# A hybrid decoder step: where value pages land, in which turn pages are requested, and where heads stand beside the key pages

## The chip, the cores and the metric

The kernel runs on one core of a Trainium2 chip. The metric is device time in microseconds (us) of one execution, from the first instruction to the end of the last. TensorE (PE) multiplies, VectorE (DVE) and ScalarE (ACT) work elementwise, GpSimd (POOL) does a little arithmetic and requests the cache pages, SyncE (SP) requests the weights; 16 DMA engines move what all of them request. Each engine runs its own instructions strictly in order and waits on semaphores.

## The reference

A decoder trunk of four layers is run for a prompt of 256 tokens and for 8 sample sequences of one token each. Layer 1 mixes tokens by block-sparse attention, layer 2 by a gated linear recurrence. Cut to what the change touches:

```
def moba_mixer(xn, pos0, w_qkv, w_o, k_pool, v_pool, li, table):
    q, k, v = jnp.split(xn @ w_qkv, 3, axis=-1)      # 8 heads of 128
    ...  # top 3 past blocks of 256 keys by q . mean(k), and the own block
    s = jnp.einsum('bqhd,bqhkld->bqhkl', qg, kg).astype(jnp.float32) * scale
    s = jnp.where(mask, s, -jnp.inf).reshape(b, qb, H, n_slots * MOBA_BLOCK)
    p = jax.nn.softmax(s, axis=-1).reshape(b, qb, H, n_slots, MOBA_BLOCK).astype(vg.dtype)
    return jnp.einsum('bqhkl,bqhkld->bqhd', p, vg)
    ...
    return out @ w_o, k, v

def rglru_mixer(xn, conv_buf, h0, w_in, conv_w, conv_b, w_a, b_a, w_x, b_x, lam, w_out):
    gate_br, x_br = jnp.split(xn @ w_in, 2, axis=-1)
    x_br, new_buf = causal_dwconv(x_br, conv_buf, conv_w, conv_b)
    r = jax.nn.sigmoid(jnp.einsum('blnc,ncd->blnd', xb, w_a) + b_a).reshape(b, L, LRU_WIDTH)
    i = jax.nn.sigmoid(jnp.einsum('blnc,ncd->blnd', xb, w_x) + b_x).reshape(b, L, LRU_WIDTH)
    a = jnp.exp(-LRU_C * r * jax.nn.softplus(-lam))
    ...  # h = a h + sqrt(1 - a^2) i x, then gelu(gate_br) * h @ w_out
```

Each sample sequence has 8 cache pages of 128 rows and 8 heads of 128, for keys and again for values: 64 key pages and 64 value pages of 0.5 MB each.

## The kernel before

**Projections.** Every weight matrix is taken in chunks of 1024 x 256 (1 MB). SP loads a chunk into one of four buffers `raw0` to `raw3`; ACT copies it to a high part `whi`, DVE subtracts to a low part `wlo` (two buffers each, `split`, L1009 and L1612); PE does 48 matmuls on it (L549 to L551). Of the output projection `wo`, chunks 0 and 1 wait in `raw0` and `raw1` and are split while the attention runs, by the two splits named `split(stage[1, "qkv"], 2, ...)`; SP loads chunks 2 and 3 into `raw2` and `raw3` after value page 31 was used.

**The sample group's attention.** Call the key pages K0 to K63 and the value pages V0 to V63, eight to a sequence. POOL requests each with one DMA (L1508) after it has read its number from the page table. A key page lands in one of the eight buffers `pg0` to `pg7`. DVE multiplies half of it by the sequence's query row and multiplies and sums the other half (`key_scores`, L1980 and L1982); ACT sums the first half in place (`key_sums`, L1215). The buffer is free when both are through (semaphores `s_kd`, `s_ka`). The query row is spread over the partitions by PE (`query`, L779); from the fifth sequence on, all share one PSUM bank, so query n waits until K(8n-1) is through. After K31 comes the first softmax (sequences 0 to 3: `scores_T`, `block_parts`, `exponentials`, `normalised`, `shares_T`, `spread`), after K63 the second. The result are the shares `pm`. PE multiplies them by four value pages at a time (`quad`, L863, 16 quads), the first eight after the first softmax, the others after the second; `s_vd` counts used value pages. `summed` and `gather` (L1251, L873) bring each half's sum into place.

**The prompt's attention** runs one head at a time beside it: `front` on PE (L832, L833; transposes of keys and values and the scores), `scores` on DVE (starts with the copy at L2061), `weigh` on ACT (L1240, L1241), `shares` on DVE (starts with L2073), `weights_T` on PE (L512 out of `sc`), `turned` on ACT (L1247), `head_sum` on PE (L848, L849), `head_out` on DVE (L2080). `front` of a head waits for `scores` of the head before.

All of this stands in an order written out by hand: for each engine a loop over the pages, with tables that say at which page which step of which head is run.

**Where value pages land before.** V0 to V31 go round eight buffers, four in `raw2` and `raw3` (`pgr`) and four of their own (`pgx`); V32 on go round the eight key buffers and the four `pgx`. POOL requests V0 to V7, then K24 to K39 without a value between them, then K40, V8, K41, V9 and so on to K63, V31, then V32 to V63 as buffers come free.

**The recurrence layer.** The input projection is 8 chunks: four for the gate branch, four for x. Behind each of the last four DVE scales the result (`XR`, L2180), convolves two tiles (L2191, L2194) and PE multiplies them by the gate weights (`gates`, L917, L918); ACT takes tanh (`gate_tanh`), DVE forms log a (`log_a`), ACT its exponentials (`decay_parts`), then DVE scans.

## Time and profile before

| | us |
|---|---|
| median of 3 runs | 2012.89 |
| lowest and highest | 2010.73, 2019.34 |
| the profiled execution | 2013.81 |
| its span of instructions | 2011.8 |

Busy shares of the span: PE 90%, DVE 66%, ACT 47%, POOL 25%. They are averages: through most of the span PE multiplies without a pause. The two stretches that the change touches are not like that. The attention runs from about 661 us (last matmul of the qkv projection) to 857.7 us (first matmul of the `wo` projection), the end of the recurrence layer's input from about 1139 to 1193 us. Times inside the trace count from the span's start.

### The profile page before, as it was taken

What the parts mean: (1) busy time and instruction counts of PE and PEld (TensorE: products, weight loads), DVE (VectorE), ACT (ScalarE), POOL (GpSimd) and SP (SyncE); (2) the same over time, 40 slices, a digit from 0 to 9 for tenths busy, and PEclk for the clock granted to TensorE, in tenths of its full rate; (3) what the DMA queues carried; (4) which work ended last, traced back from release to release, by engine and by line L of the source; (5) the groups of instructions that cost most, each with busy time, mean ns of one, the idle gap of its engine ahead of it and who ended that gap; (6) DMA issues with size and microseconds to landing.
All of it is one profiled execution on the core that took longest, in us unless ns stands there. A gap on an engine that the chain in (4) does not pass through costs nothing.

```text
span 2011.8 us, 35750 instructions
## 1 busy us (share of the span) xinstructions
PE 1807.4 (90%) x13437; PEld 1650.6 (82%) x13437; DVE 1334.8 (66%) x2470; ACT 948.6 (47%) x1713; POOL 504.1 (25%) x424
## 2 busy tenths in 40 slices
PE   4999989999999265799999859999999998999996
PEld 4999758999999121399999859999989875899996
DVE  4998796654575876465556876544799879655554
ACT  2546664453344655245434454533454666445333
POOL 2500500441120323234211005411150050144111
PEclk9999988999999667999999979999999998999998
DMA  5454494655557879955554507555546439465540
GB/s 179 132 175 135 112 264 139 195 188 169 179 172 234 324 286 387 335 161 179 177 167 154 184 2 241 185 179 170 155 135 184 134 111 265 132 199 184 180 154 22
DMA packets 317970, 365.04 MB, mean 181 GB/s; under 512 B 7802, under 2 KB 290978, under 8 KB 317750
## 3 DMA queue, kind: packets, MB, share of 16 engines
q1 hardware_dynamic: 296068, 287.41, 45.4%
q0 software_dynamic: 20560, 74.62, 10.0%
q8 instruction: 76, 1.25, 0.3%
q10 hardware_dynamic: 1216, 1.35, 0.2%
q14 instruction: 50, 0.41, 0.1%
HBM read 340.79 MB, written 23.15 MB: 181 GB/s over the span
## 4 chain that ended last, share of the span: by engine, by line
PE 62%; DVE 17%; issue 8%; ACT 5%; DVEq 3%; POOLq 2%; DMA 2%; POOL 1%; ACTq 1%; SPq 0%
PE G L549 17%; PE G L550 17%; PE G L551 17%; DVE wlo L1612 5%; ACT whi L1009 2%; DVE sums L1920 2%; PE A L512 2%; DVE xbc L1768 1%; PE A L863 1%; POOLq L1507 1%; PE A L965 1%; DVEq L1770 1%; PE G L663 1%; PE A L654 1%; DVE stx L1912 1%
## 5 line engine op out<-in xcount | busy, mean ns | idle before, releaser
L1612 DVE TENSOR_TENSOR wlo<-raw,whi 128x2048 fp32r<-128x2048 f32 x234 | 548.2, 2343 | 330.0 <-ACT whi L1009 329.9
L1009 ACT ACTIVATE whi<-raw 128x2048 fp32r<-128x2048 f32 x234 | 447.9, 1914 | 571.8 <-PE G L551 567.9
L549 PE MATMUL G<-xH,whi 128*128 128x264 f32 x2112 | 605.5, 287 | 25.6 <-DVE xL L1674 12.7
L550 PE MATMUL G<-xH,wlo 128*128 128x264 f32 x2112 | 600.3, 284 | 0.0
L551 PE MATMUL G<-xL,whi 128*128 128x264 f32 x2112 | 599.9, 284 | 0.0
L549 PEld LDWEIGHTS G<-xH,whi 128*128 128x128 f32 x2112 | 399.6, 189 | 35.7 <-issue 18.5
L550 PEld LDWEIGHTS G<-xH,wlo 128*128 128x128 f32 x2112 | 399.9, 189 | 0.1
L551 PEld LDWEIGHTS G<-xL,whi 128*128 128x128 f32 x2112 | 398.0, 188 | 0.0
L549 PE MATMUL G<-aH,whi 128*128 128x264 f32 x1024 | 292.2, 285 | 7.9 <-DVE wlo L1612 7.9
L550 PE MATMUL G<-aH,wlo 128*128 128x264 f32 x1024 | 290.7, 284 | 0.0
L551 PE MATMUL G<-aL,whi 128*128 128x264 f32 x1024 | 290.7, 284 | 0.0
L1574 POOL TENSOR_TENSOR ac<-rl 128x528 f32<-128x528 f32 x64 | 167.4, 2615 | 203.3 <-ACT rl L1343 203.3
L549 PEld LDWEIGHTS G<-aH,whi 128*128 128x128 f32 x1024 | 193.5, 189 | 9.0 <-DVE wlo L1612 9.0
L550 PEld LDWEIGHTS G<-aH,wlo 128*128 128x128 f32 x1024 | 193.7, 189 | 0.0
L551 PEld LDWEIGHTS G<-aL,whi 128*128 128x128 f32 x1024 | 192.7, 188 | 0.0
L1422 POOL TENSOR_TENSOR sums<-h 128x528 f32<-128x528 f32 x27 | 39.2, 1453 | 325.1 <-DVE xg L1664 324.8
L1420 POOL TENSOR_TENSOR sums<-h 128x528 f32<-128x528 f32 x9 | 17.5, 1945 | 362.1 <-DVE xg L1664 362.1
L1215 ACT ACTIVATE pg<-pg 128x128 f32<-128x128 f32 x256 | 75.7, 297 | 61.9 <-DVE pg L1980 60.7
L1768 DVE SCALAR_TENSOR_TENSOR xbc<-T,colC,xbc 128x256 f32<-128x256 f32 x192 | 98.4, 553 | 7.5 <-ACT xbc L1091 2.3
L2243 DVE TENSOR_TENSOR aL<-ac,aH 128x528 f32 (+1 forms) x64 | 45.3, 708 | 66.7 <-POOL ac L1574 65.6
L549 PE MATMUL G<-yH,whi 128*128 128x264 f32 x256 | 75.2, 294 | 7.8 <-DVE yL L1949 5.7
L549 PE MATMUL G<-pH,whi 128*128 128x264 f32 x256 | 75.8, 296 | 0.0
(426 smaller groups left out, 3067.1 us busy)
## 6 DMA issues: line engine op xcount, KB each, us to landing
raw<-in_mlp_w_up SPq DMA_DIRECT2D x64, 1024.0 KB, 5.3
raw<-in_mlp_w_down SPq DMA_DIRECT2D x64, 1024.0 KB, 5.1
raw<-in_ssd_w_in SPq DMA_DIRECT2D x48, 1024.0 KB, 5.4
pg<-in_cache_k POOLq DMA_DIRECT2D x64, 512.0 KB, 5.7
raw<-in_ssd_w_out SPq DMA_DIRECT2D x16, 1024.0 KB, 7.6
raw<-in_ple_w_gate SPq DMA_DIRECT2D x16, 1024.0 KB, 5.1
raw<-in_moba_w_qkv SPq DMA_DIRECT2D x12, 1024.0 KB, 5.2
pgx<-in_cache_v POOLq DMA_DIRECT2D x24, 512.0 KB, 5.9
```

The costliest lines, as they stand in the source:

```text
L512: return nc.tensor.transpose(out, in_, ident[0:k, 0:k])
L549: mm(o, whi[u % 2][:, k, w], act_h[:, x, :], start=first, stop=False)
L550: mm(o, wlo[u % 2][:, k, w], act_h[:, x, :], start=False, stop=False)
L551: done = mm(o, whi[u % 2][:, k, w], act_l[:, x, :], start=False, stop=last)
L1009: fn(whi[u % 2][:], raw[(u + 2) % 4][:], ACT.Copy).then_inc(s_hi, 1)
L1215: f = fn(pg[f"pg{j}"][:, hh, :], pg[f"pg{j}"][:, hh, :], ACT.Copy, accum_out=ms[f"sq{n % 2}"][:, j, hh:hh + 1])
L1422: gp.tensor_tensor(hh2, hr, hr, ALU.mult)
L1574: gp.tensor_tensor(ml[f"ac{b}"][:], ml[f"rl{b}"][:], ml[f"rl{b}"][:], ALU.mult).then_inc(s_ac, 1)
L1612: V.tensor_tensor(wlo[u % 2][:], raw[(u + 2) % 4][:], whi[u % 2][:].bitcast(F32), ALU.subtract).then_inc(s_lo, 1)
L1768: f = V.scalar_tensor_tensor(o, T_[:, t, k:k + SEQ], colC[:, q, ds(tile + k * CT, 1)], o, ALU.mult, ALU.add)
L1920: f = V.tensor_tensor_reduce(spare[:, (t % 8) * P:(t % 8 + 1) * P], stx[k][:, t, :], bank[t // 8][:, (t // 2 % 4) * P:(t // 2 % 4 + 1) * P ...
L2243: V.tensor_tensor(aL[:, ds(r * 2, 2), :], ml[f"ac{b}"][:], aH[:, ds(r * 2, 2), :].bitcast(F32), ALU.subtract).then_inc(s_aL, 1)
```

## The change

- Sixteen early value buffers: eight new ones, `pgw0` to `pgw7`, lie over the split buffers `whi` and `wlo`, then the four `pgr` and the four `pgx`. V0 to V47 and V56 to V63 go round these sixteen, V48 to V55 lie in the key buffers.
- Four semaphores for landed values, one for four pages, take the place of one for `pgr` and four for `pgx`.
- From K24 on POOL requests keys and values in turns: K24, V0, K25, V1 to K63, V39, then V40 to V63.
- The two early splits of `wo` stand at heads 6 and 7 and wait until V35 (ACT) and V39 (DVE) were used. SP loads chunks 2 and 3 of `wo` after V59.
- PE's order around the quads is written out anew. Five heads, not four, have their scores and shares before the second softmax; their steps stand at other pages on DVE and ACT.
- In the recurrence layer `gates` and `gate_tanh` of a pair stand one chunk later, and the first `log_a` stands behind the last convolution.

```
```diff
@@ -205,8 +206,10 @@
+        pgw = [nc.alloc_sbuf_tensor_at(f"pgw{k}", [P, MH, P], F32, offset=w0 + 4 * MH * P * k) for k in range(8)]
+        early = [t[:] for t in pgw] + pgr + [t[:] for t in pgx]
@@ -352,15 +354,9 @@
-            if t < 32:
-                turn, k = t // 8, t % 8
-                if k < 4:
-                    return pgr[k], s_pv, 64 * (turn + 1)
-                return pgx[k - 4][:], s_px[k - 4], 16 * (turn + 1)
-            turn, k = (t - 32) // RING, (t - 32) % RING
-            if k < PAGES:
-                return pg[f"pg{k}"][:], s_pg[k], 16 * (NB + turn + 1)
-            return pgx[k - PAGES][:], s_px[k - PAGES], 16 * (4 + turn + 1)
+            if 48 <= t < 56:
+                return pg[f"pg{t - 48}"][:], s_pg[t - 48], 16 * (NB + 1)
+            return early[t % 16], s_pv[t // 4 % 4], 64 * (t // 16 + 1)
@@ -472,10 +468,9 @@
-                        if hh == 3:
-                            sp.wait_ge(s_vd, 32)
-                            load_one(stage[1, "wo"], 2)
-                            load_one(stage[1, "wo"], 3)
+                    sp.wait_ge(s_vd, 60)
+                    load_one(stage[1, "wo"], 2)
+                    load_one(stage[1, "wo"], 3)
@@ -875,23 +870,52 @@
                 scores_T(0)
                 query(4)
                 shares_T(0)
-                for i in range(2 * NB):
-                    if i in (3, 5, 7, 9, 11, 13, 15):
-                        head_sum({3: 0, 5: 1, 7: 2, 9: 3, 11: 4, 13: 5, 15: 6}[i])
-                    if i in (2, 4, 6, 8, 10, 12, 14, 15):
-                        weights_T({2: 0, 4: 1, 6: 2, 8: 3, 10: 4, 12: 5, 14: 6, 15: 7}[i])
-                    if i in (1, 3, 5, 7, 9, 10, 12, 14):
-                        front({1: 0, 3: 1, 5: 2, 7: 3, 9: 4, 10: 5, 12: 6, 14: 7}[i])
-                    if i == 7:
-                        scores_T(1)
-                    if i == 8:
-                        shares_T(1)
-                    if i == 13:
-                        gather(0)
-                    quad(i)
-                    if i in (1, 3, 5):
-                        query(5 + i // 2)
-                head_sum(MH - 1)
+                quad(0)
+                front(0)
+                quad(1)
+                quad(2)
+                query(5)
+                weights_T(0)
+                quad(3)
+                head_sum(0)
+                front(1)
+                quad(4)
+                query(6)
+                weights_T(1)
+                quad(5)
+                head_sum(1)
+                front(2)
+                quad(6)
+                query(7)
+                weights_T(2)
+                quad(7)
+                head_sum(2)
+                front(3)
+                weights_T(3)
+                head_sum(3)
+                front(4)
+                weights_T(4)
+                scores_T(1)
+                head_sum(4)
+                front(5)
+                shares_T(1)
+                quad(8)
+                weights_T(5)
+                quad(9)
+                head_sum(5)
+                front(6)
+                quad(10)
+                weights_T(6)
+                quad(11)
+                head_sum(6)
+                front(7)
+                gather(0)
+                quad(12)
+                weights_T(7)
+                quad(13)
+                head_sum(7)
+                quad(14)
+                quad(15)
@@ -919,12 +943,12 @@
                 def after_in(it, u):
                     states(it, u)
-                    if not is_first(it) and u:
-                        gates(2 * u - 2)
-                        gates(2 * u - 1)
+                    if not is_first(it) and u > 1:
+                        gates(2 * u - 4)
+                        gates(2 * u - 3)
                 project(stage[2, "lru_in"], xH, xL, norm=6, after=after_in)
-                gates(KT - 2)
-                gates(KT - 1)
+                for n in range(4, KT):
+                    gates(n)
@@ -1254,21 +1278,24 @@
                     for hh in range(4):
-                        if t == (38, 46, 54, 62)[hh]:
+                        if t == (37, 42, 50, 57)[hh]:
                             weigh(hh)
-                        if t == (42, 50, 58, -1)[hh]:
+                        if t == (39, 44, 52, 59)[hh]:
                             turned(hh)
-                split(stage[1, "qkv"], 2, 2)
+                    if t == 61:
+                        weigh(4)
+                    if t == 62:
+                        turned(4)
                 exponentials(1)
-                turned(3)
-                for hh in range(4, MH):
+                for hh in range(5, MH):
                     weigh(hh)
-                    if hh == 4:
-                        split(stage[1, "qkv"], 2, 3)
                     turned(hh)
-                    if hh == 4:
+                    if hh == 5:
                         act.wait_ge(s_pr, 10)
                         summed(0)
+                    if hh > 5:
+                        act.wait_ge(s_vd, 36)
+                        split(stage[1, "qkv"], 2, hh - 4)
@@ -1308,12 +1335,14 @@
-                    if u:
-                        gate_tanh(2 * u - 2)
-                        gate_tanh(2 * u - 1)
+                    if u > 1:
+                        gate_tanh(2 * u - 4)
+                        gate_tanh(2 * u - 3)
+                gate_tanh(4)
+                gate_tanh(5)
                 decay_parts(0)
-                gate_tanh(KT - 2)
-                gate_tanh(KT - 1)
+                gate_tanh(6)
+                gate_tanh(7)
                 decay_parts(1)
...
                     act.wait_ge(s_lv, n + 1)
@@ -1513,20 +1542,13 @@
-                def value_early(turn, k):
-                    if not (isinstance(turn, int) and turn == 0):
-                        pool.wait_ge(s_vd, turn * 8 + (k - 7))
-                    buf, landed, _ = value_slot(k)
-                    page(t_in["cache_v"], turn * 8 + k, buf, landed)
-                def value_late(t):
-                    if t < 32 + PAGES:
-                        pool.wait_ge(s_kd, t + 25)
-                        pool.wait_ge(s_ka, t + 25)
-                    else:
-                        pool.wait_ge(s_vd, t - RING + 1)
+                def value_page(t):
+
+                    if 48 <= t < 56:
+                        pool.wait_ge(s_kd, t + 9)
+                        pool.wait_ge(s_ka, t + 9)
+                    elif t >= 16:
+                        pool.wait_ge(s_vd, t - 15)
                     buf, landed, _ = value_slot(t)
                     page(t_in["cache_v"], t, buf, landed)
@@ -1534,23 +1556,16 @@
                 with gp.Fori(1, 3) as it:
                     for j in range(PAGES):
                         key_page(it, j)
+                pool.wait_ge(s_mm, stage[1, "qkv"]["g0"] + 12)
                 pool.wait_ge(s_lo, stage[1, "wo"]["g0"])
-                for k in range(4):
-                    value_early(0, k)
-                pool.wait_ge(s_mm, stage[1, "qkv"]["g0"] + 12)
-                for k in range(4, 8):
-                    value_early(0, k)
-                for j in range(PAGES):
-                    key_page(3, j)
-                gp.memset(pm[:], 0.0).then_inc(s_pm, 1)
-                for j in range(PAGES):
-                    key_page(4, j)
-                with gp.Fori(1, 4) as it:
+                for n in range(3, NB):
                     for j in range(PAGES):
-                        key_page(it + 4, j)
-                        value_early(it, j)
-                for t in range(32, NB * PAGES):
-                    value_late(t)
+                        key_page(n, j)
+                        value_page(8 * (n - 3) + j)
+                    if n == 3:
+                        gp.memset(pm[:], 0.0).then_inc(s_pm, 1)
+                for t in range(40, NB * PAGES):
+                    value_page(t)
@@ -2087,25 +2102,29 @@
                     for hh in range(4):
-                        if t == (37, 45, 53, 61)[hh]:
+                        if t == (36, 41, 49, 56)[hh]:
                             scores(hh)
-                        if t == (38, 46, 54, 62)[hh]:
+                        if t == (38, 43, 51, 58)[hh]:
                             shares(hh)
-                        if t == (47, 55, -1, -1)[hh]:
+                        if t == (42, 50, 57, 60)[hh]:
                             head_out(hh)
+                    if t == 60:
+                        scores(4)
+                    if t == 62:
+                        shares(4)
                 block_parts(1)
-                head_out(2)
+                head_out(4)
+                scores(5)
                 normalised(1)
                 spread(1)
+                shares(5)
                 ov = ms["ov"][:].rearrange("p (b h) -> p b h", h=MH)
-                head_out(3)
-                for hh in range(4, MH):
+                for hh in range(6, MH):
+                    head_out(hh - 1)
                     scores(hh)
-                    if hh > 4:
-                        head_out(hh - 1)
                     shares(hh)
-                    if hh < 6:
-                        split(stage[1, "qkv"], 2, hh - 2)
+                    dve.wait_ge(s_vd, 40)
+                    split(stage[1, "qkv"], 2, hh - 4)
                 head_out(7)
@@ -2183,8 +2202,6 @@
                     if u == 0:
...
-                    if u == 3:
-                        log_a(0)
@@ -2194,6 +2211,7 @@
                 dve.drain()
+                log_a(0)
                 log_a(1)
...
```

Three places in the order. PE, behind the fourth page row of `query(5)`: L779 is the query in the kernel before, then the transposes of head 0's shares, a quad (its eight rows stand as "..."), `head_sum`, and `front(1)`. Before:

```order
L779 MATMUL A<-rowS,ident 128x512 [waits s_kd]
L779 MATMUL A<-rowS,ident 128x512
L512 MATMUL G<-ident,sc_130 128x128 [waits s_mP]
L512 MATMUL G<-ident,sc_130 128x128 x2
...
L848 MATMUL G<-pt_131,kvt_129 128x256 [waits s_mpt]
L849 MATMUL G<-pt_131,kvt_129 128x128
L512 MATMUL G<-ident,qkv 128x128 [waits s_msc]
L512 MATMUL G<-ident,qkv 128x128 x3
L832 MATMUL G<-qkv 128x128
L833 MATMUL G<-qkv 128x256
```

PE now has the same rows in the same turn, with the quad out of other buffers; only two quads, not one, stand between `front(0)` and the query. So `front(1)` stands as far behind the query as it did. What moved is its reader on DVE. DVE before, from the second key page of sequence 5 on (K41): after the copy of the sums comes K42, and `scores(1)` stands only behind K45.

```order
L1980 TENSOR_TENSOR pg_122<-pg_122,A 128x512 [waits s_pg1]
L1982 ISA pg_122,sq_154<-pg_122,A 128x128
...
L1995 COPY sS<-sq_153 128x8x8 [waits s_ka]
L1980 TENSOR_TENSOR pg_123<-pg_123,A 128x512 [waits s_pg2]
L1982 ISA pg_123,sq_154<-pg_123,A 128x128
```

DVE now, from the same page (the lines have other numbers; L2076 is the copy that begins `scores`):

```order
L1995 TENSOR_TENSOR pg_122<-pg_122,A 128x512 [waits s_pg1]
L1997 ISA pg_122,sq_154<-pg_122,A 128x128
...
L2010 COPY sS<-sq_153 128x8x8 [waits s_ka]
L2076 COPY kvt_136<-G 128x512 [waits s_mtp]
L2077 TENSOR_TENSOR sc_137<-G,amask 128x384
L2079 TENSOR_REDUCE mx_139<-sc_137 128x1
L2080 TENSOR_REDUCE mx_139<-sc_137 128x1
L2082 TENSOR_SCALAR nm_140<-mx_139 128x2
L1995 TENSOR_TENSOR pg_123<-pg_123,A 128x512 [waits s_pg2]
```

`scores(1)` stands right behind K41 and waits (`s_mtp`) for the `front(1)` that PE runs seven steps behind the query.

PE in the recurrence layer, behind the last chunk of the input projection: before, gates 4 and 5 and then 6 and 7, of which each waits for its convolution (`s_lc`).

```order
L917 MATMUL A<-xc,wax 128x264 [waits s_lth,s_lc]
L918 MATMUL A<-xc,wax 128x264
L917 MATMUL A<-xc,wax 128x264 [waits s_lth,s_lc]
L918 MATMUL A<-xc,wax 128x264
L917 MATMUL A<-xc,wax 128x264 [waits s_lth,s_lc]
```

Now gates 2 to 7 stand there in one row (twelve matmuls), 0 and 1 stand behind the chunk before, and none behind the second x chunk:

```order
L941 MATMUL A<-xc,wax 128x264 [waits s_lth,s_lc]
L942 MATMUL A<-xc,wax 128x264
L941 MATMUL A<-xc,wax 128x264 [waits s_lth,s_lc]
L942 MATMUL A<-xc,wax 128x264
L941 MATMUL A<-xc,wax 128x264 [waits s_lth,s_lc]
L942 MATMUL A<-xc,wax 128x264
```

## Rows read from the trace of the kernel before

**Rows 1.** Windows of 20 us: busy us of each engine, clock, DMA share.

```profile
core 0: us, PE busy (x) PEld busy (x) DVE busy (x) ACT busy (x) POOL busy (x), PEclk, DMA share, GB/s
700.00:720.00 20.00, 8.77 (x34) 4.29 (x38) 15.12 (x82) 11.30 (x63) 3.69 (x7) 0.50 0.61 234
...
760.00:780.00 20.00, 13.20 (x51) 4.16 (x45) 14.43 (x82) 11.22 (x70) 7.46 (x15) 0.84 1.01 390
```

**Rows 2.** Timeline of POOL's page requests (start, us, instruction, idle before): V0, K24, K40, V56.

```profile
677.21 0.53 POOL L1508 DMA_DIRECT2D raw<-in_cache_v  x1 [0.78 <-issue]
...
686.78 0.53 POOL L1508 DMA_DIRECT2D pg<-in_cache_k  x1 [0.70 <-issue]
...
717.78 0.53 POOL L1508 DMA_DIRECT2D pg<-in_cache_k  x1 [10.28 <-issue]
...
830.50 0.53 POOL L1508 DMA_DIRECT2D pg<-in_cache_v  x1 [0.64 <-issue]
```

**Rows 3.** Groups by line, 661 to 858 us: ACT's sums over key pages.

```profile
L1215 ACT ACTIVATE pg<-pg 128x128 f32<-128x128 f32 x224 | 66.2, 296 | 48.6 <-DVE pg L1980 47.8
```

**Rows 4.** Timeline of DVE: K24, first shares, K40, K41, scores(1), shares(1), K48, K63, second shares.

```profile
693.00 0.69 DVE L1980 TENSOR_TENSOR pg<-pg,A 128x512 f32<-128x512 f32 x1 [7.91 <-DMA pg<-in_cache_k]
...
718.34 0.62 DVE L2050 COPY pm<-G 128x64 f32<-128x64 f32 x4 [0.22 <-PE G L823]
...
735.67 0.69 DVE L1980 TENSOR_TENSOR pg<-pg,A 128x512 f32<-128x512 f32 x1 [3.87 <-PE A L779]
...
737.10 0.68 DVE L1980 TENSOR_TENSOR pg<-pg,A 128x512 f32<-128x512 f32 x1
...
744.54 0.68 DVE L2061 COPY kvt<-G 128x512 f32<-128x512 f32 x1
...
749.42 0.17 DVE L2073 RECIPROCAL ri<-rs 128x2 f32<-128x2 f32 x1 [1.39 <-ACT sc L1241]
...
754.80 0.69 DVE L1980 TENSOR_TENSOR pg<-pg,A 128x512 f32<-128x512 f32 x1 [2.82 <-PE A L779]
...
793.72 0.68 DVE L1980 TENSOR_TENSOR pg<-pg,A 128x512 f32<-128x512 f32 x1
...
807.98 0.61 DVE L2050 COPY pm<-A 128x64 f32<-128x64 f32 x4 [1.58 <-PE A L823]
```

**Rows 5.** Timeline of PE: scores_T(0), query(5), weights_T, quad, head_sum, front, quads, gather(1), wo.

```profile
705.94 1.89 PE L512 MATMUL G<-ident,sS 128*32 128x128 f32 x8 [28.99 <-DVEq L1989]
...
731.85 3.78 PE L779 MATMUL A<-rowS,ident 8*128 8x512 f32 x4 [6.66 <-DVE sq L1982]
735.56 0.90 PE L512 MATMUL G<-ident,sc 128*128 128x128 f32 x3
737.88 3.67 PE L863 MATMUL A<-raw,pm 128*32 128x512 f32 x16 [1.42 <-DMA raw<-in_cache_v]
741.48 1.04 PE L848 MATMUL G<-pt,kvt 128*128 128x256 f32 x2
...
743.76 1.49 PE L863 MATMUL A<-pgx,pm 128*32 128x512 f32 x6
...
815.03 1.94 PE L863 MATMUL A<-pg,pm 128*32 128x512 f32 x16
...
853.99 2.82 PE L873 MATMUL A<-headsel,vO 128*128 128x4 f32 x16 [3.57 <-ACT vO L1251]
857.74 0.59 PE L549 MATMUL G<-oH,whi 128*128 128x264 f32 x1 [0.93 <-DVE oL L2121]
```

**Rows 6.** Timeline of PE in the recurrence layer: the first gate.

```profile
1148.60 1.25 PE L917 MATMUL A<-xc,wax 128*128 128x264 f32 x2 [4.14 <-DVE xc L2194]
```

**Rows 7.** Timeline of DVE there: first and last log_a.

```profile
1166.27 1.15 DVE L2175 TENSOR_SCALAR la<-thr,ch 128x264 f32<-128x264 f32 x4
...
1175.84 0.36 DVE L2175 TENSOR_SCALAR la<-thr,ch 128x264 f32<-128x264 f32 x1 [1.40 <-ACT thi L1286]
```

**Rows 8.** Timeline of ACT there: the first of three decay instructions of the second half.

```profile
1176.23 1.08 ACT L1299 ACTIVATE thr<-la 128x1056 f32<-128x1056 f32 x1 [0.42 <-DVE la L2175]
```

4 lines of the change are left out of this document (2 added, 2 removed).

## The prediction

> **What bounds the kernel now.** I read the windows of 20 us first, then the timelines of POOL, DVE and PE between 661 and 858 us, then the end of the recurrence layer's input. Most of the span is PE multiplying, and the change doesn't touch it. Two stretches are different.
>
> In the attention a window in mid-stretch shows every DMA engine full at 390 GB/s [rows 1], so a page of 524,288 bytes costs 1.34 us of the queue. The window from 700 us has a DMA share of 0.61 and 234 GB/s [rows 1]: there POOL has nothing that it may request. It stood 10.28 us before K40, whose buffer is held by K32, and K32 waits for the first softmax [rows 2]. Further holes follow later, since V44 on want buffers that only the second half's quads free; V56, of the last eight, is requested at 830.50 [rows 2], 22 us after the second shares at 807.98 [rows 4]. DVE is the other candidate: a key page costs it 1.43 us (735.67 to 737.10), and 64 are to be done, with the heads between them [rows 4]. Its waits are the reading that matters: 7.91 us for K24, 3.87 us and 2.82 us for the query at K40 and K48 [rows 4]. Between K40 and K48 it needed 19.13 us, where the queue delivers eight keys and eight values in 16 x 1.34 = 21.4. So neither is far ahead of the other: from the first shares to K63 they take turns. Behind the second shares comes 857.74 - 808.6 = 49.1 us until `wo` begins [rows 4, 5]: four heads in a row, eight quads and the last pages.
>
> In the recurrence layer PE stands 4.14 us before the first gate [rows 6], and the last `log_a` waits for tanh at 1175.84 [rows 7].
>
> **The change part by part.** I follow each engine's turn from page to page with the durations of the rows; hand-overs between engines, 0.1 to 0.2 us, are in the differences of starts that I use.
>
> *Requests in turns from K24.* V0 to V7 no longer go ahead of K24. K24 is requested where V0 was, at 677.2 instead of 686.8 [rows 2], so the 7.91 us of DVE's wait [rows 4] go. Not all is gained: K25 to K31 now come at every second place of the queue. K24 landed as the ninth page from 677.2 at 692.9; K31 is now the fifteenth, at 692.9 + 6 x 1.34 = 701.0, so DVE ends it at 702.4. Before, it ended about 0.9 us ahead of the first transposes at 705.94 [rows 5], at 705.1. Gain 2.7 us; the first shares move from 718.3 to 715.6. K39, the 31st page, lands at 722.4, ahead of its turn.
>
> *Sixteen buffers.* V0 to V15 land in the hole before K40. From there keys and values alternate at 1.34 us each; V16 on wait for quads that PE has run long before. By this row the queue reaches V47 about 798 and V55 about 809, some 14 us ahead of the second half's quads. So the values are no longer late, and what is late next is DVE with PE.
>
> *`scores(0)` one page earlier and `shares(0)` behind K38.* The 1.39 us that DVE waits for the exponentials [rows 4] shrink to some 0.3, part of it taken by `front(0)`: 0.7 us more. The query for sequence 5 comes 2.7 + 0.7 = 3.4 us earlier and DVE starts K40 at 735.7 - 3.4 = 732.3.
>
> *`scores` right behind the query.* Here the change adds a wait. `scores(1)` stands behind K41, 2 x 1.43 + 0.1 = 3.0 us after the query. It needs `front(1)`, and PE has to run before it, at 1.2 GHz, `weights_T` 0.90, a quad 3.67, `head_sum` 1.04 [rows 5]; then `front` itself 1.2 (from the end of `head_sum` at 742.5 to 743.76). That is 6.8, with hand-overs 7.0. DVE stands 4.1 us, all key pages queued behind it. Before, `scores(1)` stood behind K45 at 744.54 and did not wait [rows 4]. The period K40 to K48 is then 19.13 - 1.39 (no wait for the exponentials) + 0.6 (the query 3.4 instead of 2.82) + 4.1 = 22.4 us. The next is the same with `scores(2)` behind K49: K56 starts at 732.3 + 2 x 22.4 = 777.1. The third hold is longer, since `scores(3)` stands behind K56 alone: 7.0 - 1.4 = 5.6. For K56 to K63 I sum 8 x 1.43 = 11.4, hold 5.6, two `scores` of 2.0 (the copy at 744.54 to the next key page), two `shares` of 0.7, two `head_out` of 0.4, the collect 0.1, and 1.6 for waits on `head_sum(3)` and `front(4)` (PE's `weights_T(3)` can only follow `shares(3)` behind K58): 24.9, with hand-overs 25.7. K63 ends at 802.8, before at 793.72 + 1.43 = 795.15: **7.6 us later**, although it started 3.4 earlier.
>
> *ACT's `turned(1)` at K44* waits for `weights_T(1)`, which PE runs only after query 6, so behind K47. The sums of K45 to K47 (four at 0.296 us, 1.18 a page [rows 3]) come 4 to 5 us late, and K53's request with them. The queue is idle as long; K53 lands about 764 and is used about 769. I cost it at nothing; the lead of 5 us is the cover.
>
> *The second softmax.* K63's end to the last copy of shares took 13.4 us (795.15 to 808.6). `scores(5)`, 2.0 us, stands where DVE waited for the exponentials, and `head_out(4)` with it: I add 1.0. Second shares at 802.8 + 14.4 = 817.2, 8.6 us later than before.
>
> *Behind it three heads, not four, and no page to wait for.* A quad costs 3.67 at 1.2 GHz and 1.94 at 2.4 GHz [rows 5]. From the shares: quad 8 3.7, `weights_T(5)` 0.9, quad 9 half and half 2.6, `head_sum` 0.9, `front(6)` 1.2, to 9.3; the DVE and ACT part of head 6, 4.2 (744.54 to 749.42, less the key page of 1.43, plus `shares` 0.7 [rows 4]), to 13.5, with quad 10 beside it; `weights_T` 0.5, quad 11 1.9, `head_sum` 0.9, `front(7)` 1.2, gather 1.8, quad 12 1.9, to 21.7; head 7's shares are ready at 23.2 because DVE's split of 2.3 us stands before its scores; `weights_T` 0.5, quad 13 1.9, `head_sum` 0.9, quads 14 and 15 3.9, to 30.4; then the copy of the sums 1.0, the gather 1.8 (2.82 before, at 1.2 GHz), and the last three small steps 2.1 with hand-overs, to 35.3. `wo` begins at 852.5, before at 857.74 [rows 5]: **gain 5.2 us**. PE comes out of it with a gap of 2 us, not 3.57 [rows 5], so I give its first chunk 1.2 us for 2.4 GHz at once (between 0 and 1.9).
>
> *Later loads of `wo`.* Chunks 2 and 3 are requested after quad 14, at about 846, and land by 852; needed from 858. Cost nothing, 5 to 6 us of cover; the two splits of chunks 0 and 1 are done by 845.
>
> *Recurrence layer.* Chunk 6 follows chunk 5 at once, 4.14 us earlier, and a `log_a` with its product, 2.3 us, leaves DVE's path before the last convolution. The convolutions end about 6 us earlier. ACT takes part back: tanh of gates 2 to 7 come in one row behind the last `XR`, and the first half's decays (three of 1.08 [rows 8]) stand before tanh 6 and 7. The last `log_a` comes at 1172.1, not 1175.84 [rows 7]: **gain 3.8 us** (2 to 6).
>
> Sum on the profiled execution: 2013.8 - 5.2 - 1.2 - 3.8 = 2003.6. It was 0.9 above the median of the runs, so 2002.7, say 2003.
>
> The Trainium skill, page "Perfetto Trace Analysis", section "Identifying the Most-Contended Engine", says to work first on the engine with the highest occupancy. In this stretch that would be the transfers, and this change would take nearly all their idle time away. That gives the third rival below, which stands on rows without it.
>
> **The rivals.**
>
> *The holds don't come* (faster). If PE reaches 2.4 GHz soon after the query, a quad is 1.94 and the whole row to `front` about 5, not 7; and DVE may be later than I think at K41. All three holds gone are 13.3 us, two thirds 9. Time 2003 - 11 = 1992. For it: the quad at 815.03 ran at 1.94. Against: at each query of the trace of before PE had stood idle for some us, 6.66 before the fifth, and its quad behind it took 3.67 [rows 5].
>
> *Clock low throughout* (slower). PE has only short bursts between DVE's and ACT's steps, so it may stay at 1.2 GHz all along: each hold grows by 1.8 (slower `front`, `query` at 3.8), and behind the second shares six quads on the path cost 1.7 more each, the two gathers 1.0 each. 5.4 + 10.2 + 2 = 17.6 over the forecast, 2020. It decides from the point where the second shares come after 827, or where the quads of the last eight take over 3 us. For it: the window from 700 us has clock 0.50 [rows 1]. Against: 1.94 in the same place of the kernel before.
>
> *The queue decides* (much faster): 104 pages from 677 at 1.34 give the last at 692.9 + 95 x 1.34 = 820, and `wo` at 827, 31 us early: 1977. Against: V56 to V63 wait for quads 10 and 11.
>
> *Nothing from the attention*: K53 to K55 land late after all (the 5 us lead used up), or chunk 2 of `wo` does, since the next weights are loaded at once behind it; either takes the 5 to 6 us. 2003 + 6 = 2009: within 0.5%.
>
> **How the numbers follow.** Forecast 0.42, its own range 1998 to 2009; no holds 0.25, at 1992; queue 0.04; nothing from the attention 0.15, at 2009; clock low 0.14, around 2020, half of it over 2023. About 0.5% (10 us) is what a measurement of this kernel tells from no change: the borders are 2002.8 and 2023. Faster: half the forecast's 0.42 and the 0.29 of the two fast rivals, 0.50. Slower: 0.08. The rest, 0.42, is within. From 1988 to 2018 leaves out the queue, the far half of the slow rival and the far edge of the fast one.
>
> **What would show it.** Right: DVE idle 3 to 6 us before the copies of `scores(1)`, `(2)`, `(3)`, released by PE's `front`; no wait for K24; V40 on requested without a hole to V55; second shares near 817; `wo` begun near 852; PE without 4.14 us before the first gate. Wrong: holds under 2 us (shares before 810, total under 1995); shares after 825; a wait of DVE on pages K53 to K56; a wait of PE on chunk 2 of `wo`.

## The result, and the profile after

The changed kernel takes 2001.85 us (median of 7 runs, 2000.76 to 2006.14), the kernel before beside it 2015.74 (7 runs, 2010.73 to 2019.34). The ratio, estimated from all runs of both kernels and not from the two medians (which alone would say 0.9931), is 0.9938, with a 95% interval of 0.9922 to 0.9953: 12.5 us less, 9 to 16. I had predicted 2003 and a gain of 10. The profiled run took 2006.14 with a span of 2004.4, the longest of the seven, so its span (7.4 under the 2011.8 of before) shows less than the ratio does.

The first timeline is that of DVE, from K27 to the second shares. Columns as in [rows 4]: start, us, instruction, and the idle time before it with what ended it.

```profile
691.47 0.69 DVE L1995 TENSOR_TENSOR pg<-pg,A 128x512 f32<-128x512 f32 x1 [1.04 <-DMA pg<-in_cache_k]
...
701.71 0.69 DVE L1995 TENSOR_TENSOR pg<-pg,A 128x512 f32<-128x512 f32 x1 [1.04 <-DMA pg<-in_cache_k]
...
716.48 0.62 DVE L2065 COPY pm<-G 128x64 f32<-128x64 f32 x4 [0.22 <-PE G L818]
...
733.31 0.69 DVE L1995 TENSOR_TENSOR pg<-pg,A 128x512 f32<-128x512 f32 x1 [3.87 <-PE A L774]
...
740.22 0.69 DVE L2076 COPY kvt<-G 128x512 f32<-128x512 f32 x1 [3.67 <-PE G L828]
...
756.14 0.69 DVE L1995 TENSOR_TENSOR pg<-pg,A 128x512 f32<-128x512 f32 x1 [3.87 <-PE A L774]
...
760.99 0.20 DVE L2010 COPY sS<-sq 128x64 f32<-128x64 f32 x1 [1.91 <-ACT pg L1239]
...
761.93 0.69 DVE L2076 COPY kvt<-G 128x512 f32<-128x512 f32 x1 [0.74 <-PE G L828]
...
784.49 0.69 DVE L2076 COPY kvt<-G 128x512 f32<-128x512 f32 x1 [5.48 <-PE G L828]
...
817.21 0.62 DVE L2065 COPY pm<-A 128x64 f32<-128x64 f32 x4 [1.58 <-PE A L818]
```

What to see: the 7.91 us before K24 in [rows 4] are gone, with five waits of 1.04 us (K27 to K31) in their place. K40 starts 2.4 us earlier (733.31, before 735.67). `scores(1)`, the first L2076 copy behind it, waits 3.67 us for PE's `front` (L828); `scores(2)` waits 0.74 behind a wait of 1.91 for ACT's sums, `scores(3)` 5.48. The second shares come at 817.21, 9.2 us later than in [rows 4].

PE's timeline around query 5 shows where 3.67 us come from:

```profile
729.50 3.77 PE L774 MATMUL A<-rowS,ident 8*128 8x512 f32 x4 [3.60 <-DVE sq L1997]
733.21 0.90 PE L507 MATMUL G<-ident,sc 128*128 128x128 f32 x3
734.03 3.66 PE L858 MATMUL A<-pgx,pm 128*32 128x512 f32 x16
737.63 1.22 PE L843 MATMUL G<-pt,kvt 128*128 128x256 f32 x2
...
739.58 0.60 PE L828 MATMUL G<-qkv 128*128 128x256 f32 x2
```

PE stands idle for 3.60 us until K39 is through, makes the query, and then does `weights_T(0)`, a quad and `head_sum(0)` before the `front(1)` for which DVE waits.

POOL's requests of V16, K53 and V56, and PE at the end of the attention:

```profile
721.59 0.53 POOL L1537 DMA_DIRECT2D pgw<-in_cache_v  x1 [4.72 <-issue]
...
759.89 0.53 POOL L1537 DMA_DIRECT2D pg<-in_cache_k  x1 [7.63 <-ACT pg L1239]
...
828.57 0.53 POOL L1537 DMA_DIRECT2D raw<-in_cache_v  x1 [18.10 <-issue]
```

```profile
848.29 1.95 PE L868 MATMUL A<-headsel,vO 128*128 128x4 f32 x16 [1.84 <-ACT vO L1275]
851.17 0.42 PE L544 MATMUL G<-oH,whi 128*128 128x264 f32 x1 [0.93 <-DVE oL L2140]
```

`wo` begins at 851.17, 6.6 us before the 857.74 of [rows 5]. From the second shares on it takes 34.0 us, before 49.8. (Both count from the start of the copies of the shares; the prediction counted from their end, 808.6 before and 817.8 now.) In the recurrence layer DVE's last `log_a` is this:

```profile
1165.36 0.36 DVE L2194 TENSOR_SCALAR la<-thr,ch 128x264 f32<-128x264 f32 x1 [0.39 <-ACT thi L1313]
```

### The profile page after: what moved, and what is told of

It reads as the page before. It is cut to its first block, busy times and chain, and to the rows that moved or that the text cites. A ratio compares the mean times of both kernels' runs of the same rounds, so it can differ in the third digit from the quotient of the medians.

```text
span 2004.4 us, 35656 instructions
## 1 busy us (share of the span) xinstructions
PE 1796.1 (90%) x13437; PEld 1649.9 (82%) x13437; DVE 1334.7 (67%) x2470; ACT 947.1 (47%) x1713; POOL 504.0 (25%) x424
## 3 DMA queue, kind: packets, MB, share of 16 engines
q8 instruction: 76, 1.25, 0.3%
## 4 chain that ended last, share of the span: by engine, by line
PE 62%; DVE 19%; issue 7%; ACT 5%; DVEq 3%; DMA 1%; POOLq 1%; ACTq 1%; POOL 0%; SPq 0%
PE G L544 17%; PE G L545 17%; PE G L546 16%; DVE wlo L1627 5%; ACT whi L1033 3%; DVE sums L1935 2%; PE A L507 2%; DVE xbc L1783 1%; PE A L989 1%; PE A L858 1%; DVE pg L1997 1%; DVE pg L1995 1%; DVEq L1785 1%; PE G L507 1%; PE G L658 1%
## 5 line engine op out<-in xcount | busy, mean ns | idle before, releaser
L544 PE MATMUL G<-xH,whi 128*128 128x264 f32 x2112 | 605.1, 286 | 26.6 <-DVE wlo L1627 13.6
L544 PEld LDWEIGHTS G<-xH,whi 128*128 128x128 f32 x2112 | 399.6, 189 | 36.6 <-issue 18.6
L544 PE MATMUL G<-aH,whi 128*128 128x264 f32 x1024 | 292.2, 285 | 8.0 <-DVE wlo L1627 8.0
L544 PEld LDWEIGHTS G<-aH,whi 128*128 128x128 f32 x1024 | 193.5, 189 | 9.1 <-DVE wlo L1627 9.0
L1239 ACT ACTIVATE pg<-pg 128x128 f32<-128x128 f32 x256 | 75.5, 297 | 48.9 <-DVE pg L1995 48.3
L544 PE MATMUL G<-yH,whi 128*128 128x264 f32 x256 | 75.3, 294 | 7.8 <-DVE yL L1964 5.7
L544 PE MATMUL G<-pH,whi 128*128 128x264 f32 x256 | 75.8, 296 | 0.0
```

Source lines behind the costliest of these rows:

```text
L544: mm(o, whi[u % 2][:, k, w], act_h[:, x, :], start=first, stop=False)
L1239: f = fn(pg[f"pg{j}"][:, hh, :], pg[f"pg{j}"][:, hh, :], ACT.Copy, accum_out=ms[f"sq{n % 2}"][:, j, hh:hh + 1])
```

## The experiments

All are compared with the kernel before, run beside them. For the attention I use two differences inside one trace, since the stretch ahead of it varies between executions (in the profiled runs query 4 starts between 670.5 and 674.9 us): the times from the start of query 4 on PE (673.17 before, 673.25 after) to the first shares, the second shares and the first matmul of `wo`. The recurrence layer's part adds nothing to them. us:

| kernel | first shares | second shares | `wo` | shares to `wo` | ratio |
|---|---|---|---|---|---|
| before | 45.2 | 134.8 | 184.6 | 49.8 | 1 |
| after | 43.2 | 144.0 | 177.9 | 34.0 | 0.9938 |
| x1, attention alone | 42.6 | 143.3 | 177.3 | 34.0 | 0.9969 |
| x2, recurrence alone | 46.0 | 135.2 | 185.5 | 50.3 | 0.9977 |
| x6, buffers and requests | 42.5 | 130.0 | 178.0 | 48.0 | 0.9954 |
| x3, turned later | 42.8 | 143.8 | 177.7 | 34.0 | 0.9949 |
| x4, fronts first | 43.1 | 134.0 | 168.9 | 34.9 | 0.9902 |
| x5, both of these | 42.8 | 133.6 | 167.7 | 34.1 | 0.9894 |
| x7, x5 with scores at query | 43.6 | 135.1 | 169.9 | 34.9 | 0.9886 |
| x8, x5 with keys first | 37.7 | 133.1 | 168.0 | 34.9 | 0.9893 |
| x9, x7 with K41, K42 ahead | 43.0 | 131.9 | 166.6 | 34.7 | 0.9870 |
| x10, x5 with the old buffers | 45.3 | 159.8 | 205.4 | 45.6 | 1.0060 |

**The two parts by themselves.** x1 is the changed kernel with the recurrence layer as before, x2 the kernel before with the recurrence layer's part of the change (gates one chunk later, both `log_a` behind the last convolution).

> The changed kernel with the recurrence layer as before, so only the attention part of the change. Theory (the parts add up): the attention stage ends 6.6 us earlier than before, as in the trace of the changed kernel (first wo matmul at 851.2 instead of 857.7 us), some 0.4 us of it is given back in the projection, and the time is 6 us under before, near 2009 where before is 2015. Rival (the recurrence part carries the gain): 0 to 2 us under before.

> The kernel before with the recurrence layer's gates and first log_a moved, and nothing else. Theory: last log_a 4.4 us earlier relative to the layer's start, as in the changed kernel (forecast 3.8), and the time 4 to 5 us under before. Rival: the gain of PE's 4.14 us wait is given back by ACT, whose tanh come in one row: under 2 us.

x1 gave 0.9969 (0.9958 to 0.9980), 6.2 us, x2 0.9977 (0.9964 to 0.9989), 4.6 us. Their product is 0.9946, within the interval of the whole change: the parts add. Inside the traces the recurrence layer gains 4.4 us: from the start of its input projection (1110.60 before, 1104.52 now, 1108.70 in x2) to the last `log_a` it takes 65.2 us before, 60.8 in the changed kernel and 60.9 in x2. One trace of each is a rough measure: in x1, whose recurrence layer is that of before, the same stretch took 67.1.

**Buffers and requests without the fifth head.** The changed kernel (its recurrence layer too) with PE's loop as before and four heads ahead of the second softmax at the places of before, on DVE and ACT. On DVE:

```
-                        if t == (36, 41, 49, 56)[hh]:
+                        if t == (37, 45, 53, 61)[hh]:
                             scores(hh)
...
-                        if t == (42, 50, 57, 60)[hh]:
+                        if t == (47, 55, -1, -1)[hh]:
                             head_out(hh)
```

> The changed kernel's sixteen buffers, requests in turns, late splits and late wo loads, and its recurrence layer, but with the order of PE's quads and heads and the pages at which DVE and ACT run the heads' steps as before (four heads ahead of the second softmax). Theory (the request part gains, the order of the heads gives part of it back): key pages end near 789 us, second shares near 802, and then four heads of about 9 us take wo to begin near 846, 5 us earlier than in the changed kernel. Rival (the fifth head ahead is what gains): wo begins at 856 or later, no better than before but for the recurrence layer.

It gave 0.9954 (0.9937 to 0.9970), and from query 4 to `wo` 178.0 us, where the changed kernel takes 177.9. The theory held up to the second shares (802.03), and missed behind them: 48.0 us, not 44, so the order of the heads gives nothing back and brings nothing. The fifth head and the new order take 14.0 us off what lies behind the second shares and put 14.0 us in front of them. So what the attention gains (0.9969 in x1) is, as far as one trace of each can tell, all from the buffers and requests; how much of it is the sixteen buffers and how much the turns of the requests was not tried apart. What they removed can be read in the trace of before: DVE waited there for the key pages K53 and K58 to K61, 4.3 us together, and PE 1.42, 4.20 and 6.90 us for the value pages of quads 2, 4 and 6. Two of these rows of DVE before:

```profile
763.49 0.69 DVE L1980 TENSOR_TENSOR pg<-pg,A 128x512 f32<-128x512 f32 x1 [1.02 <-DMA pg<-in_cache_k]
...
785.70 0.69 DVE L1980 TENSOR_TENSOR pg<-pg,A 128x512 f32<-128x512 f32 x1 [1.02 <-DMA pg<-in_cache_k]
```

Neither x6 nor the changed kernel has such a wait behind K31. In x6 2.5 us of it come back as longer waits for the queries (10.9 us, before 8.4). Its DVE rows at K48, `scores(2)` and K56 show why the front part is short: DVE waits for the queries, and next to nothing for a front.

```profile
752.16 0.69 DVE L1963 TENSOR_TENSOR pg<-pg,A 128x512 f32<-128x512 f32 x1 [3.53 <-PE A L774]
...
761.54 0.69 DVE L2044 COPY kvt<-G 128x512 f32<-128x512 f32 x1 [0.43 <-PE G L828]
...
772.88 0.69 DVE L1963 TENSOR_TENSOR pg<-pg,A 128x512 f32<-128x512 f32 x1 [3.53 <-PE A L774]
```

**The holds.** Two edits, made apart and together. x3 moves ACT's `turned(1)` and `turned(2)`, x4 moves PE's fronts (all three alike), x5 does both:

```
-                        if t == (39, 44, 52, 59)[hh]:
+                        if t == (39, 48, 56, 59)[hh]:
                             turned(hh)
```

```
                 quad(2)
+                front(1)
                 query(5)
                 weights_T(0)
                 quad(3)
                 head_sum(0)
-                front(1)
                 quad(4)
```

> The changed kernel with one number changed: ScalarE runs turned(1) and turned(2) behind K48 and K56, not K44 and K52. Theory (the delayed request of K53 has cover and costs nothing): POOL's 7.63 us gap before K53 is gone or under 2 us, DVE's starts of K48 to K63 and of the second shares (817.2) stay within 0.5 us, time that of the changed kernel, 0.994 of before (+-0.002). Rival (the late sums or the late request do set the end, over the 1.91 us that DVE waited for ScalarE at 760.99): second shares 1.5 to 2 us earlier, time 0.993 at most; half of that could not be told from the first by the median alone, so the shares' start decides.

> The changed kernel with TensorE's front(1), front(2), front(3) moved ahead of query(5), query(6), query(7); ScalarE's places left alone. Theory (the three holds are TensorE's order, each worth its length to DVE's chain): DVE's waits for front at scores(1), (2), (3), 3.67, 0.74 and 5.48 us, are gone, 9.9 us together; the waits for the query stay (3.87 each, the first shorter); the 1.91 us for ScalarE's sum at the collect of K48's sequence stays or grows, since turned(1) at K44 still blocks ScalarE while DVE is earlier. Second shares 807 to 809, wo at about 841 to 843, total 0.9890 to 0.9905 of before. Rival 1 (the earlier version with turned later as well gained through turned): second shares stay over 812, wo over 846, 0.992 or more. Rival 2 (pages set the pace once the holds go): DVE waits for key pages appear, together 3 us or more, and eat as much of the gain.

> The changed kernel with two edits: PE runs front(1), front(2), front(3) ahead of query(5), query(6), query(7) instead of behind the quad after them, and ACT's turned(1) and turned(2) stand at K48 and K56. Theory (the holds of DVE at scores cost the key pages 11.8 us: 3.7 + 2.6 + 5.5): no such waits, second shares near 806 instead of 817.8, wo begins near 840 instead of 851.2, and the time is about 11 us under the changed kernel, 24 under before. Rival (the holds only fill time in which the pages would be awaited): DVE waits for landing pages K53 to K63 instead, second shares at 813 or later, and the time is within 4 us of the changed kernel.

x3: 0.9949 (0.9932 to 0.9965), second shares 143.8 us behind query 4, not 144.0. POOL's gap of 7.63 us is gone and nothing came of it, as the theory had it; the wait of 1.91 us on ACT is gone too, but `scores(2)` now waits for `front` as long as both did before (0.74 + 1.91 = 2.65):

```profile
760.38 0.69 DVE L2076 COPY kvt<-G 128x512 f32<-128x512 f32 x1 [2.58 <-PE G L828]
```

x4: 0.9902 (0.9883 to 0.9921), second shares 10.0 us earlier, `wo` 9.0 earlier, as its theory had it; its waits for key pages behind K31 are 1.0 us. x5: 0.9894 (0.9874 to 0.9915), 1993.77 us, with 10.4 and 10.2. From the first to the second shares x5 takes 10.0 us less than the changed kernel, and DVE's waits account for it: the holds were 3.67 + 0.74 + 5.48 = 9.9 us, ACT's wait 1.91, the first query's wait shrinks by 3.87 - 2.07 = 1.8, new waits for pages take 3.2 back (0.32, 1.70, 1.21), and `front(0)` 0.2: 10.2. DVE in x5, from K40:

```profile
731.23 0.69 DVE L1995 TENSOR_TENSOR pg<-pg,A 128x512 f32<-128x512 f32 x1 [2.07 <-PE A L774]
...
734.38 0.68 DVE L2076 COPY kvt<-G 128x512 f32<-128x512 f32 x1
...
750.32 0.69 DVE L1995 TENSOR_TENSOR pg<-pg,A 128x512 f32<-128x512 f32 x1 [3.87 <-PE A L774]
...
764.43 0.69 DVE L1995 TENSOR_TENSOR pg<-pg,A 128x512 f32<-128x512 f32 x1 [1.70 <-DMA pg<-in_cache_k]
...
767.16 0.69 DVE L1995 TENSOR_TENSOR pg<-pg,A 128x512 f32<-128x512 f32 x1 [1.21 <-DMA pg<-in_cache_k]
```

`scores(1)` at 734.38 waits for nothing. PE does the front while it would stand idle for K39 anyway. But key pages are late again, as they were in the kernel before, by 0.32, 1.70 and 1.21 us.

**What sets the pace then.** x7 fills the wait for each query with a head's scores, x8 asks for K24 to K31 first, x9 is x7 with two keys ahead of V16:

```
-                        if t == (36, 41, 49, 56)[hh]:
+                        if t == (36, 39, 47, 55)[hh]:
                             scores(hh)
```

```
                         key_page(n, j)
-                        value_page(8 * (n - 3) + j)
+                        if n > 3:
+                            value_page(8 * (n - 3) + j)
+                    if n == 3:
+                        for t in range(8):
+                            value_page(t)
```

```
                         key_page(n, j)
-                        value_page(8 * (n - 3) + j)
+                        if n < 5:
+                            value_page(8 * (n - 3) + j)
+                        elif n > 5 or j >= 2:
+                            value_page(8 * (n - 3) + j - 2)
...
-                for t in range(40, NB * PAGES):
+                for t in range(38, NB * PAGES):
```

> The version with fronts ahead of the queries and turned later, and in it scores(1), (2), (3) moved on DVE from behind K41, K49, K56 to behind K39, K47, K55, so that DVE runs them while TensorE makes query 5, 6, 7. Theory (DVE's own chain sets the stretch, and the 3.87 us for each query is idle time that a head's 2.0 us of scores can fill): the waits for the query shrink from 2.07, 3.87, 3.87 to about 0 to 2, 5 to 6 us together; second shares at 806.7 - 5.5 = 801, wo at 835, total 5 us under that version's 1993.8: 1988.5. Rival (the transfers set the pace from there: that version already waited 1.70 and 1.21 us for key pages at 764 and 767, and the pairs come every 2.4 to 2.6 us): the waits move from the query to key pages K50 to K63, second shares not before 804, gain 2.5 us or less, 1991 to 1994.

> The version with fronts ahead of the queries and turned later, and in it POOL requests K24 to K31 in a row, then V0 to V7, and only from K32 on keys and values in turns. Theory (the first gain was 1.9 us and not 2.7 because K27 to K31, a pair of pages apart, land every 2.56 us, where DVE needs 1.43 us for one): the five waits of 1.04 us before K27 to K31 are gone, K31 ends 5 us earlier, the first shares start at 711, not 716; V0 to V3 have landed by then. From there all comes 5 us earlier up to the second shares if the transfers can follow, else only in part: second shares 802 to 806, total 1989 to 1993. Rival (pages are the bound from K32 on, whatever the order): first shares 711, but K32 to K39 or K50 to K63 land late, second shares 806 or more, total as that version's, 1993.8 +-1.5.

> The version with fronts ahead of the queries, turned later and scores at the query, and in its requests K41 and K42 go before V16 (from there each value page is two places later: K43, V16, K44, V17 and so on). V16 waits for quad 0, and POOL stands 4.7 to 5.2 us there with K41 behind it. Theory (the idle time of the transfers in front of V16 is what makes K45 to K47 late, which DVE waited 2.8 us for): the 2.8 us go, and part of the 4.05 us before K53 to K55; from query 4 to wo it takes 2 to 4 us less than the 169.9 us of the version without it, 166 to 168; total 1990 to 1993. Rival 1 (two requests fill nothing, since the transfers are behind by whole pages later anyway): waits for K53 to K55 stay, sum of DVE's page waits over 5 us, 169 to 170 us. Rival 2 (value pages are now late: quads wait and hold head_sum back): new waits of TensorE for value pages over 2 us, and the stretch gets longer than 170 us.

x7: 0.9886 (0.9868 to 0.9904), in the trace 2.2 us longer than x5 to `wo`. The profiled run was the longest of its four (2000.47, the median is 1994.69). My theory fell, the rival held. DVE's waits for the queries went from 9.8 us to 3.9, its waits for key pages from 3.2 to 7.3 (0.66, 1.12, 1.03 at K45 to K47, then 0.39, 1.00, 2.01, 1.04), and its waits for PE's `head_sum(1)` and `(2)` from nothing to 3.0:

```profile
745.11 0.69 DVE L1995 TENSOR_TENSOR pg<-pg,A 128x512 f32<-128x512 f32 x1 [1.12 <-DMA pg<-in_cache_k]
...
753.05 0.69 DVE L1995 TENSOR_TENSOR pg<-pg,A 128x512 f32<-128x512 f32 x1 [1.87 <-PE A L774]
...
767.07 0.69 DVE L1995 TENSOR_TENSOR pg<-pg,A 128x512 f32<-128x512 f32 x1 [2.01 <-DMA pg<-in_cache_k]
```

x8: 0.9893 (0.9876 to 0.9909). The first shares come 5.1 us earlier than in x5, as expected, and the second 0.5, so the rival held. Of the 4.6 us between, longer waits for key pages behind K31 take back 3.8 (7.1 us, such as 1.33 at 741.88 and 1.48 at 744.88; x5 has 3.2), the longer wait for query 5 1.5 (3.55, not 2.07), and `front(0)`'s 1.08 is gone. x7's windows of 20 us show the transfers without a pause; the last two columns are the DMA share and GB/s.

```profile
740.00:760.00 20.00, 10.00 (x38) 3.71 (x40) 14.71 (x82) 11.29 (x70) 8.52 (x17) 0.66 1.03 412
760.00:780.00 20.00, 11.69 (x49) 4.17 (x42) 11.69 (x63) 9.22 (x57) 8.92 (x17) 0.68 1.03 410
```

x9: 0.9870 (0.9849 to 0.9891), 1992.35 us, 166.6 us to `wo`: both numbers lie in the theory's range. The waits for K45 to K47 are gone, those for K53 to K55 (4.0 us) stay, as the first rival had it, and value pages are late, as the second had it, but the stretch doesn't get longer:

```profile
759.60 3.35 PE L858 MATMUL A<-raw,pm 128*32 128x512 f32 x16 [6.36 <-DMA raw<-in_cache_v]
```

That is quad 6; quad 7 waits another 2.32 us, `head_sum(2)` stands behind it, and DVE's `head_out(2)` waits 4.72 us for that. x5, x7, x8 and x9 can't be told apart by their intervals. All four beat both kernels of the case; I would take x5, which has the fewest edits of the four.

**The new order with the old buffers.** x5 with the slots and requests of the kernel before (twelve buffers, V0 to V7 ahead of K24, V8 on only from K40); the late splits and loads of `wo` stay.

> The version with fronts ahead of the queries and turned later (five heads ahead), but with the buffers and the order of requests of the kernel before: V0 to V7 ahead of K24, twelve buffers at most, K24 to K39 without values between them. From query 4 to wo the kernel before took 184.6 us, that version with sixteen buffers 167.7. Theory (buffers and order need each other: with the old buffers V44 to V63 can be requested only as quads 8 and on free buffers, twenty pages of 1.3 us behind the second shares): first shares 2 to 3 us later, second shares near 809, then DVE no longer sets the end but V56 to V63 do; TensorE waits for value pages at the last quads; wo 39 to 41 us after the second shares, not 34; query 4 to wo 175 to 178 us, total 0.992 to 0.995 of before. Rival 1 (the order alone brings it all): 168 to 171 us, 0.990. Rival 2 (without the buffers the order brings nothing): 182 us or more, 0.997 or more.

It gave 1.0060 (1.0039 to 1.0080), 2031.1 us, some 12 us slower than before. By its numbers this is the second rival (182 us or more, 0.997 or more), but none of the three had a loss. I had looked for it behind the second shares. Of the 37.7 us that it is longer than x5 to `wo`, 11.5 lie there, and 26.2 in front of them:

```profile
737.11 3.66 PE L865 MATMUL A<-raw,pm 128*32 128x512 f32 x16 [13.00 <-DMA raw<-in_cache_v]
...
762.80 3.67 PE L865 MATMUL A<-raw,pm 128*32 128x512 f32 x16 [12.92 <-DMA raw<-in_cache_v]
...
789.32 3.35 PE L865 MATMUL A<-raw,pm 128*32 128x512 f32 x16 [13.54 <-DMA raw<-in_cache_v]
```

```profile
744.10 0.69 DVE L2016 TENSOR_TENSOR pg<-pg,A 128x512 f32<-128x512 f32 x1 [14.72 <-PE A L781]
...
770.58 0.69 DVE L2016 TENSOR_TENSOR pg<-pg,A 128x512 f32<-128x512 f32 x1 [11.29 <-PE A L781]
...
795.87 0.69 DVE L2016 TENSOR_TENSOR pg<-pg,A 128x512 f32<-128x512 f32 x1 [10.42 <-PE A L781]
```

The new order puts quad 2 (V8 to V11) in front of query 5. With eight value buffers V8 is requested at 722.25, V11 at 730.63, and PE stands 13.00 us with the query queued behind the quad; DVE stands with it. In the changed kernel V8 to V15 are requested by 715.12, and PE waits for none of them. This is what the sixteen buffers are for in this order above all: not pages earlier at the end, but quads that PE may run ahead of a query.

## Why the prediction held, step by step

*First shares*: forecast 2.7 us earlier, measured 1.9 (716.48), by query 4 as zero the same. DVE begins K31 at 701.71, where the forecast had it land at 701.0: most of the missing part. K24 was requested at 677.83, 0.6 us behind the 677.2 that I had taken over from V0.

*V16 on*: I had them wait for quads that PE has run long before. V16 wants the buffer of V0 and waited 4.72 us for quad 0, and K41's request stood behind it (above). It cost nothing here: DVE waits for no key page behind K31.

*K40*: forecast 732.3, measured 733.31; 0.9 of the 1.0 us come from the first shares.

*The holds*: forecast 4.1, 4.1, 5.6, measured 3.67, 0.74, 5.48. The first and third and their cause, PE's row of 0.90 + 3.66 + 1.2 + `front`, are right. The second is where the step failed. DVE's collect behind K49 waits 1.91 us for ACT's late sums first, and x3 shows that this wait and the hold are one and the same time. But together they are 2.65 us, not 4.1, and in x3, without ACT's part, the hold is 2.58. The rest is PE's row, which I had at the low clock all through. Behind query 6 the granted clock rises inside the quad (0.61 in the mean from 756.9 to 759.9 us, 1.00 from there to 762): it takes 3.08 us, not 3.66, and `head_sum` begins with 0.70, not 1.22:

```profile
756.86 3.08 PE L858 MATMUL A<-pgw,pm 128*32 128x512 f32 x16
759.88 0.70 PE L843 MATMUL G<-pt,kvt 128*128 128x256 f32 x2
```

So one hold of three went the way of the rival *the holds don't come*. Against that, the wait for each query stayed at 3.87 us, where I had 3.4. The sum of the period K40 to K48 is 22.8 (forecast 22.4), of the next 21.4.

*K63*: forecast 802.8 at its end, measured 803.9 (its start at 802.50 and 1.43). *The second shares*: the forecast of 817.2 is for the end of the last copy (808.6 before). The row's 817.21 is a start; its end is 817.8. So the likeness of the two numbers means nothing: the miss is 0.6 us, 1.1 late at K63 and 0.5 less behind it.

*ACT's block at K44*: forecast 4 to 5 us, measured 7.63 at K53's request; nothing waits for K53. x3 confirms that it costs nothing.

*Behind the second shares*: forecast 35.3 from the end of the copies, measured 33.3, which makes `wo` 1.3 us earlier than 852.5. Of the quads there quad 8 (3.24) and quad 11 (2.86) were slow; each of the others took 1.94. POOL's row was not quite without a hole: V49 waited 2.98 us.

*`wo` at 2.4 GHz at once*: forecast 1.2, measured 0.2 (first evacuation 7.64 us behind the start, before 7.88). This term was mis-sized; the first matmul takes 0.42, not 0.59, but the next ones were already short before. Later in the projections 0.5 us is lost: from the start of `wo` to the first matmul of the second matrix behind it (L544, `aH`) it takes 120.6 us, before 120.1, and 120.6 in x1, x5 and x6 too. I did not look for the cause; no matmul waits for chunk 2.

*Recurrence layer*: forecast 3.8 (2 to 6). From the start of `wo` to the last `log_a` before 318.1 us [rows 5, 7], after 314.2: 3.9. The 0.5 us just named is in it: counted from the start of the layer's own input projection the gain is 4.4, in the changed kernel as in x2. The 4.14 us of [rows 6] are gone, the first gate starts at 1144.02 without a wait. x2 alone: 4.6 by the ratio.

Sum at the last `log_a`: 6.6 + 3.9 = 10.5 us, forecast 5.2 + 1.2 + 3.8 = 10.2. That the sum is so near is in part luck: the attention gave 1.4 us more than forecast, the clock at `wo` 1.0 less. The ratio says 12.5 (9 to 16), the profiled run 7.4, since in its third layer, between 1604 and 1712 us, it lost 2.5 us against the profile of before, on instructions that the change doesn't touch. x5's profile lost 0.9 there. I take it for variation between runs; no experiment was made on it.

*A reading of the kernel before that I missed*: between K40 and K63 I named only DVE's waits for the queries. Its waits for key pages there, 4.3 us (above), I left out, so my argument does not say what the new requests are worth behind K40. I also wrote that PE had stood idle for some us at each query. Ahead of query 7 it was 0.87 us, and that query took 1.98 us. And the three holds add up to 13.8, not the 13.3 of the first rival.

*The rivals.* "The holds don't come" happened at the second hold in part and not at the others; "the clock stays low" didn't happen. Nor did "nothing from the attention": neither K53 to K55 nor chunk 2 of `wo` is waited for. "The queue decides" didn't either: in the changed kernel DVE waits for no key page behind K31. The Trainium skill, page "Perfetto Trace Analysis", section "Identifying the Most-Contended Engine", would have had the busiest unit optimised first. The change did so, as the window from 700 us shows (before in [rows 1], DMA share 0.61, 234 GB/s):

```profile
700.00:720.00 20.00, 10.62 (x42) 4.50 (x42) 14.07 (x76) 10.26 (x55) 7.62 (x14) 0.50 1.03 409
```

With the buffers and requests alone (x6) that brought 6.6 us to `wo`, so far the traces agree with the Trainium skill. What paid next was an order on PE, busy 10.62 of those 20 us. Once the holds were gone DVE waited for pages again; of the two kernels that then changed the requests (x8, x9) neither can be told from x5. What the forecast did not ask is whether this order could be had without its holds.

## What to carry to other kernels

When two engines work in lockstep, look at what stands *in front* of the instruction that the other waits for: work moved into the idle time ahead of a hand-over is free, the same work behind it is paid in full (here 10.0 us up to the second shares, by moving three lines, x4). Here the fifth head didn't show its worth until that was settled (x6 against the changed kernel and x5; four heads with the fronts first were not tried). And ask of a new order which inputs it needs earlier: x5's order takes 167.7 us with the new buffers, 16.9 less than the kernel before, and 205.4 with the old ones, 20.8 more.

## What the runs showed of the hardware

PE's clock has two levels, 1.2 and 2.4 GHz, and a small block moved in front changed the level of the next. In x5, with `front(1)` ahead of it and then 2.35 us idle, query 5 took 1.98 us, at a granted clock of 1.00 (2.4 GHz); in the changed kernel, after 3.60 us idle, 3.77 (above), at 0.50 (1.2 GHz), and the quad behind it still 3.66. It was the same in x4, x7 and x9, which have `front(1)` in front (1.98 after 2.36 us), and in x1 and x3, which don't (3.78 and 3.77 after 3.60). In x8, with `front(1)` in front but 3.66 us idle behind it, query 5 took 3.46.

```profile
729.21 1.98 PE L774 MATMUL A<-rowS,ident 8*128 8x512 f32 x4 [2.35 <-DVE sq L1997]
```

So moving the front gave 1.8 us more at K40 (a wait of 2.07, not 3.87). At query 6 and 7 the idle time in x5 was 7.35 and 8.88 us, and they took 3.78 and 3.77.

In mid-stretch a key and a value page together take 2.56 us, 1,048,576 bytes, 410 GB/s, and windows in x5 and x7 show 410 to 412; [rows 1] had 390, from which I took 1.34 us a page. The Trainium skill, page "DMA: Bandwidth & Descriptors", section "Where 436 GB/s comes from", names about 358 GB/s, half of what the memory gives two cores, as the limit of the memory side for such transfers, and 435 as that of the fabric. This program runs on one core, and its 410 GB/s were above the first. No run here has a second core loading beside it.
